# The memory's keys and values at the start of a two-block transformer kernel instead of at its end

## The reference

```python
# first block
mod_x = silu(c) @ ada_w + ada_b          # 1024 -> 6144, one row; the same with c_ctx
sh1, sc1, g1, sh2, sc2, g2 = split(mod_x)
hx = rmsnorm(x, norm1_g) * (1 + sc1) + sh1       # 512 x 1024
hc = rmsnorm(ctx, norm1_g) * (1 + csc1) + csh1   # 256 x 1024
px = hx @ w_in ; pc = hc @ w_in                  # and then attention, Fourier mixing, MLP
# second block: mixer, band attention, w_o, and then
kk, vv = split(rmsnorm(mem, norm_mem) @ w_mkv)   # mem: 256 x 1024, w_mkv: 1024 x 2048
q = rmsnorm(x, norm_xattn) @ w_mq                # 4 heads of width 256
x = x + softmax(q kk^T / 16) vv @ w_mo
```

## Time and profile before

| | |
|---|---|
| Median of 3 runs | 2285.01 us (2282.09 to 2285.64) |
| Profiled execution | 2293.44 us, its span 2291.6 us |
| PE busy | 2199.8 us, 96% |
| PEld, DVE, ACT, POOL busy | 1819.5, 892.9, 830.5, 884.7 us |
| Granted PE clock, mean | 0.979 of full speed |
| Read from DRAM, written | 198.01 MB, 6.29 MB |

### The profile page before, as it was taken

One profiled execution on the slowest core, in us unless ns is written; L12 is line 12 of the kernel. 1 busy time (PEld: TensorE's weight loads), 2 busy tenths in 40 slices (PEclk: granted clock), 3 DMA queues, 4 the chain that ended last, 5 costly groups with the idle time before them and its releaser, 6 DMA issues.

```text
span 2291.6 us, 28699 instructions
## 1 busy us (share of the span) xinstructions
PE 2199.8 (96%) x11528; PEld 1819.5 (79%) x11528; DVE 892.9 (39%) x1411; ACT 830.5 (36%) x1208; POOL 884.7 (39%) x640
## 2 busy tenths in 40 slices
PE   6999999989999989999999999999999999999998
PEld 3766678868888868979797878787888988888887
DVE  2357945441211246574756410505144244222102
ACT  2446533232322335242424413636233443222212
POOL 0324964434445434031221244131354524444442
PEclk8999989999999999999999999999999999999998
DMA  6411334422332233020211133131232412223221
GB/s 219 164 55 56 111 122 129 147 74 95 99 101 92 92 113 97 19 74 19 92 38 37 37 103 97 39 102 41 99 117 85 148 56 92 92 92 105 96 92 55
DMA packets 179968, 205.89 MB, mean 90 GB/s; under 512 B 3364, under 2 KB 170768, under 8 KB 179472
## 3 DMA queue, kind: packets, MB, share of 16 engines
q1 hardware_dynamic: 176912, 195.17, 26.3%
q10 hardware_dynamic: 2944, 9.15, 1.1%
HBM read 198.01 MB, written 6.29 MB: 89 GB/s over the span
## 4 chain that ended last, share of the span: by engine, by line
PE 80%; DVE 6%; POOL 5%; ACT 2%; issue 1%; DMA 1%; DVEq 0%; ACTq 0%; SPq 0%; POOLq 0%
PE ps L2071 20%; PE ps L2073 20%; PE ps L2072 20%; PE ps L2180 3%; PE ps L2599 2%; POOL raw L705 2%; PE ps L2612 2%; POOL raw L707 2%; POOL w_lo L688 2%; PE ps L2683 2%; PE ps L2700 1%; PE ps L2118 1%; PE ps L2120 1%; PE ps L2119 1%; ACT w_hi L760 1%
## 5 line engine op out<-in xcount | busy, mean ns | idle before, releaser
L688 POOL TENSOR_TENSOR w_lo<-raw,w_hi 128x512 fp32r<-128x512 f32 x586 | 781.2, 1365 | 1342.3 <-ACT w_hi L760 1342.3
L2071 PE MATMUL ps<-h_hi,w_hi 128*128 128x512 f32 x1384 | 560.3, 405 | 13.6 <-DVE h_lo L1410 4.4
L2073 PE MATMUL ps<-h_hi,w_lo 128*128 128x512 f32 x1384 | 544.2, 393 | 0.0
L2072 PE MATMUL ps<-h_lo,w_hi 128*128 128x512 f32 x1384 | 543.7, 393 | 0.0
L760 ACT ACTIVATE w_hi<-raw 128x2048 fp32r<-128x2048 f32 x150 | 285.7, 1905 | 373.5 <-PE ps L2073 365.4
L2071 PEld LDWEIGHTS ps<-h_hi,w_hi 128*128 128x128 f32 x1384 | 262.6, 190 | 74.8 <-issue 10.7
L2073 PEld LDWEIGHTS ps<-h_hi,w_lo 128*128 128x128 f32 x1384 | 262.6, 190 | 56.6
L2072 PEld LDWEIGHTS ps<-h_lo,w_hi 128*128 128x128 f32 x1384 | 263.0, 190 | 52.8 <-issue 1.5
L2071 PE MATMUL ps<-g_hi,w_hi 128*128 128x512 f32 x256 | 101.0, 394 | 0.0
L2073 PE MATMUL ps<-g_hi,w_lo 128*128 128x512 f32 x256 | 100.4, 392 | 0.0
L2072 PE MATMUL ps<-g_lo,w_hi 128*128 128x512 f32 x256 | 99.4, 388 | 0.0
(11 more groups left out here) (417 smaller groups left out, 3830.2 us busy)
## 6 DMA issues: line engine op xcount, KB each, us to landing
raw<-w_in SPq DMA_DIRECT2D x48, 1024.0 KB, 5.3
raw<-w_down SPq DMA_DIRECT2D x27, 1024.0 KB, 5.1
raw<-ada_w SPq DMA_DIRECT2D x24, 1024.0 KB, 5.2
raw<-w_gate_up SPq DMA_DIRECT2D x22, 1024.0 KB, 5.0
raw<-w_up SPq DMA_DIRECT2D x16, 1024.0 KB, 5.4
raw<-w_mkv SPq DMA_DIRECT2D x8, 1024.0 KB, 5.3
raw<-w_out SPq DMA_DIRECT2D x4, 1024.0 KB, 5.7
xT<-bias_band SPq DMA_DIRECT2D x2, 2048.0 KB, 10.0
```

The costliest lines, as they stand in the source:

```text
L688: ins = nc.gpsimd.tensor_tensor(w_lo[:, split_at[u] % 2, cols], raw[:, u % 2, cols], w_hi[:, split_at[u] % 2, cols].bitcast(F32), ALU.subt ...
L2071: T.matmul(out_, wh, hi, start=start, stop=False, skip_group_check=True)
L2072: T.matmul(out_, wh, lo, start=False, stop=False, skip_group_check=True)
L2073: return T.matmul(out_, wl, hi, start=False, stop=stop, skip_group_check=True)
```

## The change

The memory moves to the head of the program. Its eight units come first in `units`, before `lat_q`; all eight share the low half between POOL and DVE. The eight modulation units leave the list of units: each has a buffer of its own (`ada_raw`), placed over memory that is free at that time, and a `pick` matrix of the constants takes the place of the identity in `ada_turn`. The products of a modulation unit go to four groups of 32 columns of the array: k-tile k writes to the 32 PSUM partitions of group k mod 4, and the turn adds the four. Keys and values are evicted to `mk_out` and `mv_out`, written to DRAM (`m_kept`), and loaded again (`m_kT`, `m_v`) before the query units. In the memory stage the memory's load, turns, norm and products are gone, and the last query unit takes the place of the last value unit between the second and third score items.

```diff
+    ADA_SRC = [block(t["ada_w"], 0, KT, 256 * b, 256) for b in ADA_BLOCK]
+    for j in range(8):
+        wide("mkv", "mkv", t["w_mkv_2"], 0, 256 * j, 0)
+    wide("lat_q", "q", t["w_in"], 0, FOUR_W, 2)
...
+    X_BANK = [2, 3, 5, 7]
+    ADA_BEFORE = {0: (0, 1), 1: (2,), 2: (3,), 3: (4,), 4: (5,), 5: (6,), 6: (7,)}
...   # SP
+            sp.dma_start(m_in[:, :, :], t["mem_2"]...).then_inc(sem["table_in"], 16)
+            def load_ada(a):
+                if a >= 6:
+                    sp.wait_ge(sem["tr_done"], 2 * KT)
+                sp.dma_start(ada_raw[a][:, :]..., ADA_SRC[a]).then_inc(ada_in[a // 2], 16)
+            load(mkv)
+            load_ada(0)
+            load(mkv + 1)
+            for a in range(1, 6):
+                load_ada(a)
+            load(mkv + 2)
+            load_ada(6)
+            load(mkv + 3)
+            load_ada(7)
...   # SP, before the query units
-            sp.wait_ge(sem["y_lo_done"], 16)
-            sp.dma_start(m_in[:, :, :], t["mem_2"]...)
+            sp.wait_ge(sem["tile_done"], tile_count(gated("bout", "proj", 3), 1))
+            sp.dma_start(m_kT[:, :, :]..., m_kept[:, 0:KT * C]).then_inc(sem["table_in"], 16)
+            sp.dma_start(m_v[:, :, :]..., m_kept[:, KT * C:]).then_inc(sem["table_in"], 16)
...   # ACT
+            table_of_sqrt()
             for k in range(KT):
+                act.wait_ge(sem["xt_done"], k // 2 + 1)
+                squares(N_MEM, k, m_T[:, k, :])
+            next_hi()
+            std_of(N_MEM, 1.0 / D, 2)
+            norm_hi(N_MEM, m_hi, None)
+            next_hi()
+            def store_memory(j):
+                for jj in range(2):
+                    act.wait_ge(sem["mkv_mm"], 2 * j + jj + 1)
+                    nc.scalar.activation(dst, ps[:, 2 + jj, 0:256], ACT.Copy).then_inc(sem["mem_stored"], 1)
+            ada_rows(0)
+            ada_rows(1)
+            for k in range(KT):
+                squares(N_X, k, xT[:, k, :])
+            for j in range(8):
+                next_hi()
+                store_memory(j)
+                if j == 0:
+                    for i in range(4):     # copies of the turned context, two tiles each
+                if j == 1:
+                    std_of(N_X, 1.0 / D)
                     for k in range(KT):
                         squares(N_CTX, k, cT[:, k, :])
+                if j == 2:
                     std_of(N_CTX, 1.0 / D, 2)
+                if 4 <= j <= 6:
+                    act.wait_ge(sem["ada_mod"], j + 1)
+                    norm_hi(N_X, h_hi, ..., range(2 * (j - 4), 2 * (j - 3)))
+                if j == 6:
+                    norm_hi(N_X, h_hi, ..., range(6, KT))
+                for a in ADA_BEFORE.get(j + 1, ()):
+                    ada_rows(a)
             act.dma_start(x_kept, ...)
+            act.wait_ge(sem["mem_stored"], 16)
+            act.dma_start(m_kept[:, 0:KT * C], ...)
+            act.dma_start(m_kept[:, KT * C:], ...)
...   # DVE
+            lower_half(0)
+            inverse_of(N_MEM, 2)
+            normed(N_MEM, m_T, ...)
+            lower_half(1)
             for k in range(KT):
                 add_square(N_X, k)
+            ada_cols(0)
+            lower_half(2)
+            ada_cols(1)
+            lower_half(3)
+            inverse_of(N_X)
+            for k in range(KT):
+                add_square(N_CTX, k, C)
+            ada_cols(2)
+            lower_half(4)
             inverse_of(N_CTX, 2)
+            ada_cols(3)
+            lower_half(5)
...   # PE
             def ada_mm(a):
+                pe.wait_ge(ada_in[a // 2], 32)
                 for k in range(KT):
+                    rows = slice(32 * (k % 4), 32 * (k % 4 + 1))
+                    ins = T.matmul(ps[rows, a % 2, 0:256], silu_wide[:, k, :],
+                                   ada_raw[a][:, k * 256:(k + 1) * 256], start=k < 4, stop=k >= 4, ...)
+            norm_sum(N_MEM, 2)
+            for j in range(8):
+                for a in ADA_BEFORE.get(j, ()):
                     ada_mm(a)
+                if j == 0:
+                    spread(N_MEM, 2)
+                if j == 2:
+                    spread(N_X)
+                    norm_sum(N_CTX, 2)
+                if j == 3:
+                    spread(N_CTX, 2)
+                memory_gemm(j)       # waits for mem_stored of unit j - 1, half by half
+                for a in ADA_BEFORE.get(j, ()):
+                    ada_turn(a)
+                if j == 0:           # turns of the context, the second half behind ACT's copies
+                if j == 1:
+                    norm_sum(N_X)
...   # PE, memory stage
+            wide_gemm(u + 2, h_hi, h_lo)
+            pe.wait_ge(sem["table_in"], 80)
+            stored([u])
+            def last_queries():
+                wide_gemm(first["mq"] + 3, h_hi, h_lo)
+                stored(range(first["mq"] + 1, first["mq"] + 4))
+            attention("mem", (), last_queries)
```

More of the change, by code:

```diff
@@ L172, in build @@
     w_qb = r("w_qb", [P, 2, H1 * QK1])
+    ADA_AT = [h_hi_at, h_hi_at + 4 * UNIT, h_lo_at, qk_tok_at, c_hi_at, c_lo_at, BASE, BASE + 4 * UNIT]
+    ada_raw = [r.over(f"ada_raw{i}", [P, UNIT], at_) for i, at_ in enumerate(ADA_AT)]
     r = Region(60 * 1024)
@@ L436, in build @@
     w_in_slot = [nc.alloc_semaphore(f"w_in_slot{i}") for i in range(2)]
+    ada_in = [nc.alloc_semaphore(f"ada_in{i}") for i in range(4)]
     bank_stored = {i: nc.alloc_semaphore(f"bank_stored{i}") for i in (0, 1, 2, 3, 6, 7)}
@@ L479, in slot_before @@
         return old[0] if len(old) == 2 else None
-    shared_lo = list(range(first["mkv"] + 2, first["mkv"] + 8))
+    shared_lo = list(range(first["mkv"], first["mkv"] + 8))
     def lo_half_count(u):
@@ L756, in hi_of @@
                     act.wait_ge(sem["w_mm_done"], old - first["down2"] + 1)
+                elif old is not None and units[old].kind == "mkv":
+                    act.wait_ge(sem["mkv_mm"], 2 * (old - first["mkv"]) + 2)
                 elif old is not None:
@@ L2200, in _ @@
             pe.wait_ge(sem["vec_done"], 1)
+            pe.wait_ge(sem["table_in"], 16)
+            for k in range(KT):
+                if k >= 4:
+                    pe.wait_ge(sem["xt_done"], k // 2 - 1)
+                for tt in range(2):
+                    at_ = (k % 2) * C + tt * P
+                    ins = turn(ps[:, 4 + 2 * (k % 4 // 2), at_:at_ + P], m_in[:, tt, k * P:(k + 1) * P])
+                ins.then_inc(sem["tr_done"], 1)
             pe.wait_ge(sem["x_in_done"], 16)
@@ L2245, in ctx_there @@
             def ctx_there():
-                pe.wait_ge(sem["n_lo"], 16)
+                pe.wait_ge(sem["n_lo"], 8 * NORM_INDEX[N_CTX] + 8)
             u = first["lat_kv"]
-            wide_gemm(first["lat_q"], h_hi, h_lo, ready=after(sem["n_lo"], 0))
             pe.wait_ge(sem["ada_mod"], 8)
+            wide_gemm(first["lat_q"], h_hi, h_lo, ready=after(sem["n_lo"], 8 * NORM_INDEX[N_X]))
+            pe.wait_ge(sem["mem_stored"], 16)
             wide_gemm(first["f0"], h_hi, h_lo)
@@ L2509, in _ @@
             u = first["ab"]
-            gemm(u, [([(k * P, h_hi[:, k, :], h_lo[:, k, :]) for k in range(KT)], S)], ready=after(sem["n_lo"], 24))
+            gemm(u, [([(k * P, h_hi[:, k, :], h_lo[:, k, :]) for k in range(KT)], S)], ready=after(sem["n_lo"], 8 * NORM_INDEX[N_MIX]))
             pe.wait_ge(bank_stored[bank_of(u, 0)], stored_count(u, 0))
@@ L2746, in _ @@
             out_phase("out2", y2_hi, y2_lo, after(sem["y_lo_done"], 8), N_XATTN)
-            def turn_memory(ks):
-                for k in ks:
-                    if k >= 4:
-                        pe.wait_ge(sem["m_T_done"], k - 3)
-                    for tt in range(2):
-                        ins = turn(ps[:, 4 + k % 4, tok(tt)], m_in[:, tt, k * P:(k + 1) * P])
-                    ins.then_inc(sem["m_tr"], 1)
             u = first["mq"]
-            wide_gemm(u, h_hi, h_lo, ready=after(sem["n_lo"], 32))
+            wide_gemm(u, h_hi, h_lo, ready=after(sem["n_lo"], 8 * NORM_INDEX[N_XATTN]))
             norm_sum(N_XATTN)
```

343 lines of the change are left out of this document (153 added, 190 removed).

## The result

The changed kernel takes 2305.54 us (median of 4 runs, 2304.27 to 2309.62) against 2285.32 for the kernel before (4 runs). The ratio is 1.0087, 95% interval 1.0067 to 1.0106: slower by 20 us. The forecast was 2287.7 us, +2.7, and the time lies above its range. The profiled execution took 2305.45 us, equal to its median; that of before took 2293.44, 8 above its own. So the two traces show 12.1 us of the 20 (spans of 2303.7 and 2291.6).

What follows compares the result with a forecast made beforehand. TensorE (PE) was taken to bound the kernel. Head +55.9, f0's wait -1.6 and late part -51.6 gave +2.7 us: 2287.7 on the median 2285.0. Own range 2281 to 2291; 8 in 10, 2278 to 2302.

Steps and rivals of the forecast that it cites:

- Semaphore renumbering, the other banks of the norm sums and the root table loaded earlier cost nothing: Side effects of the change, priced at nothing beside the loads at the start.
- Head: Before the first wide product: the added memory units delay it from 69.89 to 125.8 us, +55.9.
- rounds: Head, memory units 3 to 7: 8.2 us from start to start, ACT splitting unit j+2 before evicting unit j.
- The estimate of 1.0 for a modulation unit in four groups: Head: a modulation unit, now 3.61 us, takes 1.0 in four column groups; 0.9 at best, 3.6 at worst.
- rival C: Head: column groups run one after another or give no overlap, 3.6 us each; +13.6, 2301.3 us; chance 0.11.
- D: Rival, head: more ACT waits in the chain of units 0 to 2, half their idle again; +6, 2294 us; chance 0.11.
- The clock fell where it was charged: Head: three slow-clock charges after PE idle gaps, 1.9, 1.8 and 1.9 us, 5.6 in all.
- Rival B: Head: the clock falls in the gaps of the rounds too; +8.5 if all fall, 2296.2 us; chance 0.18.
- rival A: Head packs tighter, without the three clock charges (5.6) and the contention (2.5); net -5.4, 2279.6 us; chance 0.24.
- Just behind the head: After the first wide product: f0's wait of 1.56 us goes, its split running under lat_q; -1.6.
- the stores: Just behind the head: storing the 4 MB kept in DRAM, late at about 142 against 148 us, costs nothing.
- Late part: Memory stage: products of keys and values removed, third scores start at 1781.2 instead of 1832.82 us; 51.6 saved.

Runs made afterwards that it cites:

- e5: The changed kernel once more, unedited, beside the kernel before on one chip: 2305.88 us, ratio 1.0076 [1.0052, 1.0100].
- its own experiment: Changed kernel with 160 spare bytes, a modulation unit's eight products all into rows 0 to 31, one after another: 2300.53 us, ratio 1.0048.

## Why the prediction was wrong

The medians of kernels with the same start of the stage tensors give the change by itself:

| start modulo 256 | without the change | with it | difference |
|---|---|---|---|
| 128 | 2282.3 | 2292.6 | +10.3 |
| 192 | 2289.0 | 2294.2 | +5.2 |
| 0 | 2295.4 | 2301.4 | +6.0 |
| 224 (different chips) | 2295.9 | 2305.9 | +10.0 |

So the change costs some 5 to 10 us by itself where the sum gave +2.7. Each difference can be off by some 5 us, so one pair alone (at 192, ratio 1.0016 [1.0001, 1.0032]) would not rule the +2.7 out; all four lie above it. And its 32 bytes cost about 9 more (8.9 in the traces; 6 to 12 between medians of one version at 192 and at the slow starts).

**The step that failed** is the sentence "Semaphore renumbering, the other banks of the norm sums and the root table loaded earlier cost nothing", or rather what is missing from it: `pick`, two more columns of constants, was priced nowhere. The diff shows `CONST_N` growing ahead of every stage tensor, and the earlier trace rows show only products of `h`, so nothing that I had read told `h` from `g`. The trace of before had it in the units, 10.99 us for `g` and 10.88 for `h`; the means by form did not show it, 394, 392 and 388 ns for `g` beside 393 and 393 for the second and third products of `h`, because the mean of `h` also holds products at the lower clock. It is nearly half of the 20 us.

The Trainium skill's page "SBUF — State Buffer", section "Operand start alignment", asks only that an operand start at a multiple of its element size, and says that this is about legality. All starts here meet it, and the step still differs. The Trainium skill's page "TensorE: Matmul & The Clock Gate", section "Wait — 56ns, not 53.3ns?", gives 215.7 ns from start to start for 512 columns, back to back; the best seen here is 226.7, at start 128, so the trace does not agree. What makes the difference between the starts no run here shows.

**Head, +55.9 predicted, +56.6 measured.** Every step landed within 2 us: end of the spread 35.06 (34.8), the hole of 5.91 (6), unit 1 at 58.24 (60.1), unit 2 at 74.30 (75.7), rounds of 8.36 (8.2), first query product 126.53 (125.8). The estimate of 1.0 for a modulation unit in four groups came out at 1.07, so rival C fell, also by its own experiment; D's further waits in units 0 to 2 did not appear. The clock fell where it was charged, and twice more: unit 0 ran at 0.60 between 36 and 44 us, which ACT's longer chain hid, and unit 3 at 0.72 between 85 and 91 us, behind a wait of 2.15 that I had charged nothing, and took back the 1.4 us that the chain was ahead by. Rival B, the clock falling in the rounds, did not happen in this trace (1.00 from 92 to 126); rival A's tighter packing did not either.

That the head fits to 0.7 us is in part luck. The first query product stands at 67.8, 68.1, 68.4, 69.1 and 69.9 us in the five traces of the kernel before and its shifted versions (its products read only `h`, so the shift does not touch them), and 69.89, on which the sum was made, is the latest. With the change it stands between 126.4 and 129.3 in six traces, 128.0 in the middle. So the head costs some 59.6 us and not 56.6.

**Just behind the head, -1.6.** f0's wait went, but the stores were "nothing" only for f0. The load of lat_kv was late beside them, and 0.9 us came back. At lat_kv's split the head stood at +55.7 (predicted 54.3). The middle of the six traces less the middle of the five (142.5 and 85.2) is +57.3.

**Late part, -51.6 predicted, -50.1 measured.** The third scores wait 1.05 for DVE's product, as worked out; what is short is the clock. mq+2 starts behind a wait of 2.10 us instead of 1.24, and its first product takes 0.77 instead of 0.50; the window of the changed kernel stands at 0.88 (12% of 14 us is 1.7), where the kernel before was at 1.00. I had charged nothing.

```profile
1815.00:1829.00 14.00, 13.11 (x51) 10.74 (x52) 0.93 (x2) 1.05 (x2) 5.81 (x5) 0.88 0.44 150
```

That fall of the clock is itself a matter of the execution. In e5, the changed kernel once more, the first product takes 0.50 and the stretch is 24.9 us long, as forecast (1781.2 less 1756.27):

```profile
1817.42 0.50 PE L2133 MATMUL ps<-h_hi,w_hi 128*128 128x512 f32 x1 [2.10 <-POOL w_lo L721]
...
1842.30 1.10 PE L2453 MATMUL ps<-m_kT,m_q 128*128 128x256 f32 x4 [1.05 <-DVE m_q L2064]
```

Of the six traces with the change and the old order of ScalarE, two have 24.9 and four 26.5. The stretch before the change lasts 75.2 to 76.55 us in five traces, 75.6 in the middle, and again the sum was made on the longest. So 49 to 51 us are saved.

These add up: 57.3 less 49.2 (the middle ones, 75.6 and 26.5) is +8.1, inside the table's +5 to +10. Of the 5.4 us above the forecast's +2.7, 2.4 come from the one trace that served as the start of the sum (1.5 in the head, 0.9 late), 1.5 from the clock late, and the rest from the head and the late load.

By the two first traces, 55.7 less 50.1 plus 8.9 is 14.5 against 12.1. The trace of before lost the difference, and 1 us more, between lat_kv and 171 us: from lat_kv's split to the fifth behind it pass 84.5 us there and 81.0 in the changed kernel, and part of that stage ran at these clocks, before (0.76) and after (1.00).

```profile
136.00:150.00 14.00, 11.08 (x37) 7.62 (x36) 9.93 (x15) 5.64 (x10) 3.58 (x3) 0.76 0.25 75
192.00:206.00 14.00, 11.08 (x53) 8.30 (x52) 10.04 (x17) 6.78 (x11) 3.31 (x3) 1.00 0.26 77
```

**The range** was built from the bounds of the ada unit and the clock, and had no term for the placement. With its 9 us in the sum the forecast would have been 2297; the remaining 9 us to 2305.5 are the 2 to 7 us by which the change itself was undersized, and scatter that the runs do not resolve.

## What to carry to other kernels

When a change adds a constant or a buffer ahead of others, work out which tensors move, compare the lengths of equal units of work that read different tensors (a mean over all of a group's products can hide the difference behind the clock), and price a difference of a few ns times the number of products; then time the old kernel at the new placement before judging the change (here 192 unused bytes gave 0.31%). Where a sum is made on one trace, look whether another execution has the same length of the stretch: here both stretches were the longest of five. Work moved from a stage that TensorE bounds into one where it waits is only free if what ends those waits has room: here ScalarE and VectorE bound the head, and the 45 us of products taken out late came back early, in full.

## What the runs showed of the hardware

The step of a 512-column matmul of this kernel, mean of the three products of a tile, goes by where its moving operand starts:

| start modulo 256 | step, ns | unit of 48, us |
|---|---|---|
| 128 | 226.7 | 10.88 |
| 192 | 228.9 | 10.99 |
| 160, 224, 0, 64 | 233.3 | 11.20 |

Only 192 was seen at two starts 256 bytes apart. 32 and 96 were not tried, nor was a move of the weights' side or of `h`. The weights start at 128 throughout, so whether the start itself counts or its distance from theirs stays open. And the three products differ: at 192 the one that reads `g_lo` takes 388 ns, no more than at 128 (389), the other two 394 and 392, so the start alone does not fix the step of a single product.

Four groups of 32 columns ran eight products of 256 columns in 1.07 us against 3.64 one after another, 3.4 times as fast; by the starts alone (a set of four every 216 ns, against one) it is four times.
